# Two transformer blocks in float32, one core: reordering the loads and the first step at the opening

## What is computed

```python
cs = jax.nn.silu(c)
mod = (cs @ mod_w[layer] + mod_b[layer]).reshape(bsz, N_SUB, 3, D_MODEL)
# each sublayer:
y = f(x * (1 + scale) + shift)
x = layer_norm(ALPHA * x + (1 + gate) * y, ln_g, ln_b)
# the feed-forward ones have
f = lambda u: 0.5 * (silu(u @ w_gate) * (u @ w_up)) @ w_down      # 1024 -> 2816 -> 1024
```

## Time and profile before

| | |
|---|---|
| median of 3 runs | 1659.3 us (1658.55 to 1662.34) |
| profiled execution, its own time | 1656.16 us |
| its span, first to last instruction | 1654.2 us |
| PE, DVE, ACT busy | 1472.4, 1158.5, 870.7 us |
| TensorE clock granted, mean | 0.944 |
| read from HBM | 303.91 MB |

### The profile page before, as it was taken

How to read it: one execution, slowest core, us unless ns; L and a number is a source line. 1 busy time by engine, 2 the same in 40 slices (tenths; PEclk the granted TensorE clock), 3 DMA queues, 4 the chain that set the end, 5 groups by cost and what they waited for, 6 DMA issues and landing times. The chain is left out here.

```text
span 1654.2 us, 23359 instructions
## 1 busy us (share of the span) xinstructions
PE 1472.4 (89%) x8783; PEld 1260.6 (76%) x8783; DVE 1158.5 (70%) x2080; ACT 870.7 (53%) x1606; POOL 0.2 (0%) x4
## 2 busy tenths in 40 slices
PE   3999999996979999999998568899997997799887
PEld 2888879886858888788887565688886994599745
DVE  5988878868659888788888455786677345454364
ACT  1554454552446445564544447655555965485463
POOL 0000000000000000000000000000000000000000
PEclk9999999998979999999999789999998998799987
DMA  9899768530036897578784160395556440546000
GB/s 368 316 327 330 278 208 270 175 115 1 1 102 229 299 338 242 177 270 327 280 297 142 42 241 1 105 313 189 185 162 214 154 171 1 153 125 195 40 1 26
DMA packets 197515, 306.46 MB, mean 185 GB/s; under 512 B 10562, under 2 KB 159132, under 8 KB 197404
## 3 DMA queue, kind: packets, MB, share of 16 engines
q1 hardware_dynamic: 195744, 303.55, 53.9%
q10 hardware_dynamic: 1660, 1.43, 0.3%
HBM read 303.91 MB, written 1.05 MB: 184 GB/s over the span
## 5 line engine op out<-in xcount | busy, mean ns | idle before, releaser
L926 PE MATMUL bank<-u_hi_lo,w_hi 128*128 128x512 f32 x1344 | 473.8, 397 | 12.2 <-DVE arena L988 12.2
L925 PE MATMUL bank<-u_hi_lo,w_lo 128*128 128x256 f32 x1176 | 328.6, 279 | 0.0
L977 DVE TENSOR_TENSOR w_lo<-weight_ring,w_hi 128x1024 fp32r<-128x1024 f32 x264 | 307.8, 1220 | 12.0 <-ACT w_hi L947 11.3
L926 PEld LDWEIGHTS bank<-u_hi_lo,w_hi 128*128 128x128 f32 x1344 | 246.8, 188 | 63.7 <-DVE arena L988 15.1
L947 ACT CAST w_hi<-weight_ring 128x1024 fp32r<-128x1024 f32 x264 | 260.3, 1047 | 11.2 <-DMA weight_ring<-in_ffn_w_up_dram 5.5
L925 PEld LDWEIGHTS bank<-u_hi_lo,w_lo 128*128 128x128 f32 x1176 | 222.5, 189 | 7.4
L1197 DVE TENSOR_TENSOR wp_lo<-weight_ring,wp_hi 128x1024 fp32r<-128x1024 f32 (+4 forms) x149 | 167.7, 1164 | 59.1 <-ACT wp_hi L1164 58.8
L848 PE MATMUL bank<-src_hi,wp_hi 128*128 128x256 f32 (+1 forms) x632 | 183.1, 300 | 0.5 <-ACT src_hi L434 0.3
L1164 ACT CAST wp_hi<-weight_ring 128x1024 fp32r<-128x1024 f32 (+4 forms) x149 | 143.8, 1008 | 62.8 <-PE bank L848 56.5
L848 PE MATMUL bank<-src_lo,wp_hi 128*128 128x256 f32 (+1 forms) x632 | 173.6, 286 | 0.0
L848 PE MATMUL bank<-src_hi,wp_lo 128*128 128x256 f32 (+1 forms) x632 | 173.5, 286 | 0.0
(11 more groups left out here) (358 smaller groups left out, 2209.4 us busy)
## 6 DMA issues: line engine op xcount, KB each, us to landing
weight_ring<-in_mod_w_dram SPq DMA_DIRECT2D x72, 1024.0 KB, 6.9
weight_ring<-in_ffn_w_gate_dram SPq DMA_DIRECT2D x44, 1024.0 KB, 6.0
weight_ring<-in_ffn_w_up_dram SPq DMA_DIRECT2D x44, 1024.0 KB, 5.5
weight_ring<-in_ffn_w_down_dram SPq DMA_DIRECT2D x44, 1024.0 KB, 8.3
weight_ring<-in_hyb_w_in_dram SPq DMA_DIRECT2D x16, 1024.0 KB, 8.2
weight_ring<-in_w_in_e_dram SPq DMA_DIRECT2D x16, 1024.0 KB, 5.5
weight_ring<-in_w_in_o_dram SPq DMA_DIRECT2D x13, 1024.0 KB, 5.7
weight_ring<-in_hyb_w_out_dram SPq DMA_DIRECT2D x4, 1024.0 KB, 4.8
```

The costliest lines, as they stand in the source:

```text
L925: nc.tensor.matmul(bank[:, 0:SEQ], w[1], u[:, 0:SEQ], start=False, stop=False, skip_group_check=True)
L926: last = nc.tensor.matmul(bank[:, :], w[0], u, start=kt == 0, stop=kt == KT - 1, skip_group_check=True)
L977: nc.vector.tensor_tensor(part_view(wl, n, part), raw, part_view(wh, n, part).bitcast(F32), ALU.subtract).then_inc(w_lo.sem, w_lo.up())
```

## The change

- ACT loads only the identity columns of the tables at the start. The rest of the tables, `pos_row`, `pos_col` and `phi_w2` move to the SP queue, ahead of tile 21, in front of the five row vectors (`late_inputs`, twelve transfers in place of five).
- `x_tok` is issued ahead of tile 8 instead of tile 6, so behind all eight modulation tiles.
- SP waits, ahead of tiles 8, 9 and 10, until tiles 3, 5 and 7 have landed.
- In the opening, the gate weights of step 0 are split ahead of the wait for the modulation columns, the up weights behind chunk 1. `Opening` gets `scalar_chunks = (2, 3)`.
- `LayerNorm` gets `first_banks = (4, 5)`: step 0 puts gate and up into banks 4 and 5, and step 1 doesn't wait for the sums of step 0. `Opening` keeps banks 0 and 1 and the wait.
- At the end of the first feed-forward DVE waits until all late inputs are in.

```diff
-            for i, (dst, src) in enumerate([(tab[:, :], D["tables"])] +
+            for i, (dst, src) in enumerate([(tab[:, 0:P], D["tables"][:, 0:P])] +
...
-            for i in range(3):
-                load(phi_w2[:, i, :], D["phi_w2_2"][0, i // 2])
-            load(pos_row[:, :], D["positions"][0, :].partition_broadcast(P))
-            for a in range(TT):
-                load(pos_col[:, a:a + 1], D["positions"][0, a * P:(a + 1) * P].rearrange("(p o) -> p o", o=1))
+        def late_inputs():
+
+            pos = D["positions"][0]
+            out = [(tab[:, P:ntab], D["tables"][:, P:ntab]), (pos_row[:, :], pos.partition_broadcast(P))]
+            out += [(pos_col[:, a:a + 1], pos[a * P:(a + 1) * P].rearrange("(p o) -> p o", o=1)) for a in range(TT)]
+            out += [(phi_w2[:, i, :], D["phi_w2_2"][0, i // 2]) for i in range(3)]
+            return out + [(bc[key], src.partition_broadcast(P)) for key, src in row_vectors]
...
             banks = (2, 3, 4, 5)
-            scalar_chunks = ()
+            first_banks = (0, 1)
+            scalar_chunks = (2, 3)
...
             def act(self, act, split_hi, hi):
+                split_hi(0, 0)
                 act.wait_ge(mod_taken.sem, 2)
                 for c in range(4):
                     self.high(act, hi, c)
-                    if c == 0:
-                        split_hi(0)
+                    if c == 1:
+                        split_hi(0, 1)
+                self.floats(act)
 
             def dve(self, dve, split_lo, hi, lo):
+                split_lo(0, 0)
                 dve.wait_ge(mod_done.sem, 2)
                 for u in range(2):
                     mod_take(dve, u)
                 for c in range(4):
                     self.low(dve, hi, lo, c)
-                    if c == 0:
-                        split_lo(0)
+                    if c == 1:
+                        split_lo(0, 1)
...
             banks = (2, 3, 6, 7)
-            scalar_chunks = (2, 3)
+            first_banks = (4, 5)
...
+            def gate_up_bank(j, part):
+
+                return PB[part if j else head.first_banks[part]]
...
+                if not m:
+                    dve.wait_ge(inputs_in, 16 * len(late_inputs()))
                 dve.drain().then_inc(stage_done.sem, stage_done.up())
...
-                        if part < 2:
+                        if part < 2 and (j > 1 or head.first_banks[part] == part):
                             summed = up_summed if part else gate_summed
                             pe.wait_ge(summed.sem, summed.base + j)
...
+            ahead = {8: 3, 9: 5, 10: 7}
             for n, tile in enumerate(plan):
                 if n == 3 * RING:
-                    for key, src in row_vectors:
-                        sp.dma_start(bc[key], src.partition_broadcast(P)).then_inc(inputs_in, 16)
+                    for dst, src in late_inputs():
+                        sp.dma_start(dst, src).then_inc(inputs_in, 16)
                 if n >= RING:
                     sp.wait_ge(*plan[n - RING].freed)
-                if n == RING - 1:
+                if n in ahead:
+                    sp.wait_ge(loaded[plan[ahead[n]].slot], plan[ahead[n]].need)
+                if n == len(first_mods):
                     sp.dma_start(x_tok, D["x"].rearrange("b (a p) d -> p (b a) d", p=P)).then_inc(x_in, 16)
```

More of the change, by code:

```diff
@@ L231, in two_blocks_kernel @@
         rows = arena.take(3 * P, "p (a d) -> p a d", a=3)
-        in_count, first_count = [0], [0]
+        first_count = [0]
         def row_groups():
@@ L259, in _ @@
         def _(act):
-            def load(dst, src):
-                act.dma_start(dst, src).then_inc(inputs_in, 16)
-                in_count[0] += 16
             act.dma_start(csT[:, :], D["c"].rearrange("b (p r) -> p (b r)", p=P)).then_inc(c_in, 16)
-            for i, (dst, src) in enumerate([(tab[:, :], D["tables"])] +
+            for i, (dst, src) in enumerate([(tab[:, 0:P], D["tables"][:, 0:P])] +
                                            [(rows[r:r + src.shape[0], a, :], src) for a, r, src in row_groups()] +
@@ L954, in _ @@
                         act.wait_ge(gate_summed.sem, gate_summed.base + j)
-                    nc.scalar.copy(part_lo[:, 0, :], PB[0][:, SEQ:2 * SEQ]).then_inc(gate_half.sem, gate_half.up())
+                    nc.scalar.copy(part_lo[:, 0, :], gate_up_bank(j, 0)[:, SEQ:2 * SEQ]).then_inc(gate_half.sem, gate_half.up())
                     act.wait_ge(w_used.sem, w_used.base + up_n[j] + 1)
@@ L958, in _ @@
                         act.wait_ge(up_summed.sem, up_summed.base + j)
-                    nc.scalar.copy(part_lo[:, 1, :], PB[1][:, SEQ:2 * SEQ]).then_inc(up_half.sem, up_half.up())
+                    nc.scalar.copy(part_lo[:, 1, :], gate_up_bank(j, 1)[:, SEQ:2 * SEQ]).then_inc(up_half.sem, up_half.up())
                     act.wait_ge(gate_summed.sem, gate_summed.base + j + 1)
@@ L972, in _, with split_lo @@
                 head.begin(dve)
-                def split_lo(j):
-                    for n, part, jj, tile, raw in steps[j]:
+                def split_lo(j, one=None):
+                    for n, part, jj, tile, raw in steps[j] if one is None else steps[j][one:one + 1]:
                         dve.wait_ge(w_hi.sem, w_hi.base + n + 1)
@@ L987, in _ @@
                         dve.wait_ge(hf_ready.sem, hf_ready.base + j - 1)
-                    nc.vector.tensor_tensor(e[:, j % 2, :], PB[0][:, 0:SEQ], part_lo[:, 0, :], ALU.add) \
+                    nc.vector.tensor_tensor(e[:, j % 2, :], gate_up_bank(j, 0)[:, 0:SEQ], part_lo[:, 0, :], ALU.add) \
                         .then_inc(gate_summed.sem, gate_summed.up())
                     dve.wait_ge(up_half.sem, up_half.base + j + 1)
-                    nc.vector.tensor_tensor(uf[:, j % 2, :], PB[1][:, 0:SEQ], part_lo[:, 1, :], ALU.add) \
+                    nc.vector.tensor_tensor(uf[:, j % 2, :], gate_up_bank(j, 1)[:, 0:SEQ], part_lo[:, 1, :], ALU.add) \
                         .then_inc(up_summed.sem, up_summed.up())
@@ L1028, in first_step @@
                             for kt in (2 * c, 2 * c + 1):
-                                nc.tensor.matmul(PB[part][:, 0:SEQ], hi[:, kt, :], uh[:, kt, :], start=kt == 0,
+                                nc.tensor.matmul(gate_up_bank(0, part)[:, 0:SEQ], hi[:, kt, :], uh[:, kt, :], start=kt == 0,
                                                  stop=False, skip_group_check=True)
@@ L1033, in first_step @@
                         for kt in range(KT):
-                            nc.tensor.matmul(PB[part][:, 0:SEQ], lo[:, kt, :], uh[:, kt, :], start=False, stop=False,
+                            nc.tensor.matmul(gate_up_bank(0, part)[:, 0:SEQ], lo[:, kt, :], uh[:, kt, :], start=False, stop=False,
                                              skip_group_check=True)
@@ L1039, in first_step @@
                             for kt in (2 * c, 2 * c + 1):
-                                last = nc.tensor.matmul(PB[part][:, SEQ:2 * SEQ], hi[:, kt, :], ul[:, kt, :], start=False,
+                                last = nc.tensor.matmul(gate_up_bank(0, part)[:, SEQ:2 * SEQ], hi[:, kt, :], ul[:, kt, :], start=False,
                                                         stop=kt == KT - 1, skip_group_check=True)
@@ L1835, in gate_inputs @@
                 dve.wait_ge(small_ready.sem, small_ready.base + 2)
-                dve.wait_ge(inputs_in, in_count[0] + 16 * len(row_vectors))
+                dve.wait_ge(inputs_in, 16 * len(late_inputs()))
                 nc.vector.tensor_scalar(iw8, small[:, :, 0:8], 8.0 ** -0.5, None, ALU.mult)
```

## The result

| | before | after |
|---|---|---|
| median | 1659.7 us (6 runs, 1655.9 to 1662.3) | 1649.2 us (6 runs, 1645.8 to 1655.3) |
| profiled execution, its own time | 1656.16 us | 1647.69 us |
| its span | 1654.2 us | 1645.9 us |
| PE, DVE, ACT busy | 1472.4, 1158.5, 870.7 us | 1467.0, 1155.9, 871.7 us |
| granted clock, mean | 0.944 | 0.946 |

The changed kernel takes 0.9944 of the time before, 95% interval [0.992, 0.9967]: 9.3 us less, between 5.5 and 13.3.

A forecast was written before the change was run, and what follows sets the result against it. PE sets the pace in the first feed-forward; bytes ahead of the last modulation tile and tokens bound the opening. 5.4 + 3.4 - 6.05 = 2.8 us off 1659.3 gives 1656.5; own range 1654.5 to 1658.5, over all cases 1651.5 to 1661.5.

The forecast's parts named there:

- Opening up to the columns: Start to modulation columns: tokens land at 26.8, columns ready at 34.6, 3.3 us earlier; bounds 1.8 and 5.0.
- My 3.58: Opening, second reduction on PE: assumed to take 3.58 us as before, with 1.84 as the faster bound.
- my 5.4: Whole opening: step 1 of the first feed-forward starts at 46.3, earlier by 5.4 us.
- Columns to step 1: Opening, modulation columns to step 1: 11.7 us instead of 13.8, with ACT as the longer chain; 2.1 us won.
- Heads: Other feed-forwards' heads: PE's wait ahead of step 1 goes, step 2 still waits for DVE; 3.4 us won, bounds 2.1 and 6.2.
- Late inputs: Twelve transfers ahead of tile 21 on SP's queue: delay reaches PE by step 7, first feed-forward loses 6.05 us.
- D: Added time ahead of tile 21 on SP's queue: 6.2 us, bounds 3.8 and 9.3.
- Rival 1: SP's queue: small loads cost next to nothing, D = 3.8, gain 5.2 us, 1654.1; chance 0.31.
- rival 2: SP's queue: all five small loads stall it 1.3 us each, D = 9.3, gain about none, 1659.6; chance 0.20.
- The rule of ring order: DMA queues: an engine takes one queue's descriptors in ring order; said to speak against moving the late inputs; no size.

The follow-up runs named there:

- e9: Changed kernel with late inputs singly ahead of every second tile from 22, tables in four parts, tokens ahead of the last modulation tile; 1646.8 us median, ratio 0.9919.
- e1_banks_only: Kernel before, with only the other banks for step 0 in the three LayerNorm heads; 1652.8 us median, ratio 0.9978.
- e7: Changed kernel with `pos_row`, two `pos_col` and three `phi_w2` ahead of tile 45, tables and five row vectors ahead of tile 21; 1648.1 us, one run.
- e4: Changed kernel with the two 2 KB vectors `a_log` and `dt_bias` ahead of tile 45, the other ten late inputs ahead of tile 21; 1646.9 us, one run.
- e5: As e4, plus four loads of 16 bytes per partition from one address, ahead of tile 21 into unused memory; 1659.0 us, one run.
- e6: As e4, plus four loads of 16 bytes per partition from 128 addresses, ahead of tile 21 into unused memory; 1644.9 us, one run.
- e13_before_fourth: Kernel before, unchanged, profiled a fourth time; 1661.4 us.
- e2: Changed kernel with late inputs issued one at a time ahead of every second tile from tile 22 on, tables in four parts; 1646.6 us median, ratio 0.993.
- e10: Changed kernel, unchanged, profiled once more; 1651.4 us, one run.

## Why the prediction was wrong

The direction was right, and so was most of the mechanism. The price of the late inputs was too large, because I took the wrong thing for what makes a short load dear, and one term was missing. Of the 6.5 us between 2.8 and 9.3:

1. **Opening up to the columns** (3.3 predicted): 37.85 - 33.60 = 4.25. The tokens landed near 27.4, between my 26.8 and 28.3. The reduction ran straight behind the transposes, as expected, but in 2.24 us, of which I had named 1.84 as a bound. Over the eight other profiles with this opening (e9 apart, where the tokens come earlier) the lead at step 1 is 5.0 to 5.6 in the six with a reduction of 3.41 us, and 6.5 in the two in which the clock rose on the way. My 3.58 and my 5.4 fit the more frequent case; the first profile was among the better, and its extra 0.9 is luck of the execution.
2. **Columns to step 1** (11.7 predicted): 45.36 - 33.60 = 11.76. Right. With the term above the opening gave 6.3 instead of 5.4: 0.9 more.
3. **Heads** (3.4 predicted, 0.7 + 2.05 + 0.7): 0.7 + 2.2 + 0.7 = 3.7 after and in e1_banks_only. Right, with step 2 as the next to wait, and at 499 my 0.4 from sum to product was 0.40.
4. **Late inputs** (6.05 lost predicted): 3.9 lost in the first profile, 2.7 to 4.5 over four. This is the step that failed. The path to PE was right: step 7 hangs on tile 24 with no wait for PE between, and 0.25 us of slack stood where I had 0.15. The price D was wrong. I had 2.35 for the tables and 3.85 for the six small loads. The runs give 1.6 (e7) and 1.0 to 1.7. The error is in the two `pos_col`, which I held nearest to the two 2 KB vectors and gave 1.3 each: they landed 0.21 to 0.39 behind the load before them. The row on the two vectors was read rightly, as e4 (1.4 to 1.75 us) and e5 (1.7) show; what I took for its cause, short pieces, was not. Pieces of 16 bytes that come from one address cost 1.7 us a load, the same from 128 addresses 0.3 (e6). `pos_col` has 128 addresses. Rival 1, with D = 3.8 and 0.2 for each of `pos_col` and `phi_w2`, had the size and the kind. The rule on short transfers that rival 2 cited, from the Trainium skill's page "DMA: Bandwidth & Descriptors", section "Specifications", does not give the price of a load here: 2 KB in some 0.3 us (e6) is 7 GB/s, so far off the 385 to 416 of the opening as the rule has it, but the same pieces from one address took five to six times as long (e5).
5. **Second block** (nothing predicted): the kernels with the new banks take 2.1 to 2.8 us less behind the last product, in either group. I put it at nothing, and the profile before gives no row to price it from. It goes with less time at the lower level of the clock; why there is less of it is not shown. The 3.1 us between the profile before and its median, which I had noted, are explained: that profile was in the short group of the rest, the other three were not. The sum was taken off the median, so they did no harm.

Sum for the first profile, whose rest is 2.2 shorter: 0.9 + 0.3 + 2.1 + 2.2 = 5.5 of the 6.5. Since the landing of tile 24 sets the lead behind step 7, terms 1 and 4 belong together: I had 5.4 - 6.05 = -0.65 at the end of the first feed-forward, and it is 2.0 to 2.7, some 3 us more, the largest part of the miss. The rest is within what single profiles differ by: 1.6 at one step in e13_before_fourth. From the profiles alone, the mean span is 1657.2 over four before and 1648.0 over three after, 9.2 us apart, which agrees with the ratio.

The rule of ring order that I cited from the Trainium skill's page "DMA: Bandwidth & Descriptors", section "Queues, rings and completion order", agrees with the traces: issued in front of tile 21, the late inputs delay it, and spread behind it (e2) they let it land at 68.81 and delay no tile that is waited for. The best versions by median are e2_spread and e9_spread_tokens_eighth, 2.6 and 2.4 us under the changed kernel's median, with intervals that overlap its own; the lead at the end of the first feed-forward, 5.2 and 6.5 against 2.0 to 2.7, says that the gain is real.

## What to carry to other kernels

Price a load of a few bytes per partition by whether all partitions read one address, and not by its bytes (`pos_row`, 1 KB to each partition from one address, landed 0.30 to 0.33 us behind the load before it). Put loads that nobody waits for between the weight tiles and not in one block ahead of a late one. Read a transfer's price from when the tile behind it lands, since a lead that the transfers take away anyway hides it. When a gain is read from two traces, profile each kernel more than once: a stretch with little PE work moved by 3 us between executions of one program, more than most terms of such a sum. A bank that the first step leaves free pays only up to the next wait on the same chain, here 3.7 us of 6.2.

## What the hardware showed

- A load of 16 bytes to each of 128 partitions from one address delayed the tiles behind it by 1.4 to 1.75 us (e4, e5), while the transfers of the core fell to 1 to 65 GB/s and the DMA engines to a busy share of 0.03 (e7); the same bytes from 128 addresses delayed them by 0.3 us (e6). Why one address is slow, the traces don't say.
- The sixteen narrow matmuls of the reduction took 2.24 us in one execution of the changed kernel and 3.41 in another (e10). They start 0.213 or 0.112 us apart, and in the first the change from one to the other falls on the trace's first record of the clock, at 31.7.
- One program's profiled span varied by 5.3 us (before, four) and 3.7 us (after, three) with no wait changed: at 52 to 56 with a granted clock of 0.60 instead of 1.00, and in an 80 us window of the second block with 0.75 instead of 0.81.
